# Four of twelve normalisation factors taken to all rows through memory instead of by PE's products and DVE's copy

## The reference

```python
def rms_norm(x, g, eps=EPS):
    xf = x.astype(jnp.float32)
    y = xf * lax.rsqrt(jnp.mean(xf * xf, axis=-1, keepdims=True) + eps)
    return (y * g.astype(jnp.float32)).astype(x.dtype)

def sq_relu_mlp(hn, w_up, w_down):
    return jnp.square(jax.nn.relu(hn @ w_up)) @ w_down
...
    ckv = hn @ w_dkv                                  # mla_shared_kv, hn = rms_norm(h, kv_in_norm_g)
    c, k_rope = ckv[..., :KV_LORA], ckv[..., KV_LORA:]
    kv = (rms_norm(c, kv_norm_g) @ w_ukv).reshape(B, S, MLA_HEADS, MLA_NOPE + MLA_V)
...
    cq = rms_norm(hn @ w_dq, q_norm_g)                # mla_attention
    q = (cq @ w_uq).reshape(B, S, H, MLA_NOPE + MLA_ROPE)
...
        h = h + sq_relu_mlp(rms_norm(h, mlp_norm_g[l]), w_up[l], w_down[l])
```

## Time and profile before

| | us |
|---|---|
| median of 3 runs | 1815.76 (1815.21 to 1815.92) |
| the profiled execution, its own time | 1815.61 |
| its span, first to last instruction | 1813.5 |
| PE busy | 1799.1 (99% of the span) |
| DVE busy | 879.6 (48%) |
| ACT busy | 623.7 (34%) |
| POOL busy | 536.9 (30%) |

### The profile page before, as it was taken

How to read it: one execution, slowest core, us unless ns; L and a number is a source line. 1 busy time by engine, 2 the same in 40 slices (tenths; PEclk the granted TensorE clock), 3 DMA queues, 4 the chain that set the end, 5 groups by cost and what they waited for, 6 DMA issues and landing times.

```text
span 1813.5 us, 21889 instructions
## 1 busy us (share of the span) xinstructions
PE 1799.1 (99%) x8494; PEld 1462.4 (81%) x8496; DVE 879.6 (48%) x1223; ACT 623.7 (34%) x916; POOL 536.9 (30%) x340
## 2 busy tenths in 40 slices
PE   9999999999999999999999999999999999999999
PEld 8877788888888887788888888877677888888877
DVE  6556563333334767553333334479655422333357
ACT  4344532222222345422222224334645332221244
POOL 1222254132325530153232225423222220210232
PEclk9999999999999999999999999999999999999999
DMA  5322222222322234325222322322122222232222
GB/s 211 108 84 78 75 93 93 93 93 93 104 97 100 79 108 131 111 93 128 93 93 94 114 93 89 115 81 70 55 92 97 93 93 93 93 116 86 100 95 92
DMA packets 37058, 177.70 MB, mean 98 GB/s; under 512 B 4569, under 2 KB 11513, under 8 KB 18041
## 3 DMA queue, kind: packets, MB, share of 16 engines
q1 hardware_dynamic: 35808, 175.06, 28.7%
q10 hardware_dynamic: 1176, 1.63, 0.7%
HBM read 161.99 MB, written 3.67 MB: 91 GB/s over the span
## 4 chain that ended last, share of the span: by engine, by line
PE 88%; DVE 8%; ACT 2%; issue 1%; POOL 1%; DMA 0%; SPq 0%; DVEq 0%; ACTq 0%; POOLq 0%
PE ps L564 23%; PE ps L565 22%; PE ps L566 22%; PE ps L619 3%; PE ps L618 3%; PE ps L596 3%; PE ps L830 1%; PE ps L792 1%; DVE wlo L1751 1%; PE ps L841 1%; DVE idx_score L2223 1%; DVE top L2221 1%; PE ps L638 1%; PE ps L1010 1%; PE ps L1020 1%
## 5 line engine op out<-in xcount | busy, mean ns | idle before, releaser
L1751 DVE TENSOR_TENSOR wlo<-raw,whi 128x2048 fp32r<-128x2048 f32 x133 | 325.8, 2449 | 301.6 <-ACT whi L1249 301.1
L564 PE MATMUL ps<-xb,whi 128*128 128x512 f32 (+1 forms) x996 | 388.4, 390 | 1.4 <-ACT probs L1553 0.8
L566 PE MATMUL ps<-xb,wlo 128*128 128x512 f32 (+1 forms) x996 | 386.1, 388 | 0.0
L565 PE MATMUL ps<-xb,whi 128*128 128x512 f32 (+1 forms) x996 | 386.1, 388 | 0.0
L1249 ACT ACTIVATE whi<-raw 128x2048 fp32r<-128x2048 f32 x143 | 273.0, 1909 | 324.6 <-PE ps L566 248.9
L564 PE MATMUL ps<-xa_hi,whi 128*128 128x512 f32 x788 | 308.5, 391 | 0.7 <-ACT probs L1318 0.7
L566 PE MATMUL ps<-xa_hi,wlo 128*128 128x512 f32 x788 | 306.8, 389 | 0.0
L565 PE MATMUL ps<-xa_lo,whi 128*128 128x512 f32 x788 | 306.7, 389 | 0.0
L564 PEld LDWEIGHTS ps<-xb,whi 128*128 128x128 f32 x996 | 187.1, 188 | 43.6 <-issue 5.0
L566 PEld LDWEIGHTS ps<-xb,wlo 128*128 128x128 f32 x996 | 187.0, 188 | 38.6
L565 PEld LDWEIGHTS ps<-xb,whi 128*128 128x128 f32 x996 | 187.1, 188 | 37.4
(11 more groups left out here) (332 smaller groups left out, 2428.3 us busy)
## 6 DMA issues: line engine op xcount, KB each, us to landing
raw<-wst SPq DMA_DIRECT2D x148, 1024.0 KB, 4.8
stage<-qk_raw SPq DMA_DIRECT2D x32, 128.0 KB, 2.3
mla_qn<-q_nope SPq DMA_DIRECT2D x8, 256.0 KB, 2.4
mla_v<-v_tok SPq DMA_DIRECT2D x8, 256.0 KB, 2.7
outT<-h SPq DMA_DIRECT2D x7, 256.0 KB, 2.0
h<-xT SPq DMA_DIRECT2D x3, 512.0 KB, 7.4
bias_scratch<-bias_rows ACTq DMA_DIRECT2D x1, 1536.0 KB
raw<-wst SPq DMA_DIRECT2D x4, 256.0 KB, 6.0
```

Of the source, the lines that this page charges most:

```text
L564: pe.matmul(out, lhs_hi, rhs_hi, start=first, stop=False)
L565: pe.matmul(out, lhs_hi, rhs_lo, start=False, stop=False)
L566: return pe.matmul(out, lhs_lo, rhs_hi, start=False, stop=last)
L1751: dve.tensor_tensor(wlo[slot][:, :], raw[slot][:, :], whi[slot][:, :].bitcast(F32), ALU.subtract).then_inc(wlo_done, 1)
```

## The change

For norms 1, 2, 4 and 5, `broadcast` is left out of PE's list and `take_rstd` out of DVE's. In their place ACT begins two transfers, with a wait ahead of each: `factor_away(n)` waits for `rstd_t` of norm n and writes its 128 x 4 numbers to 512 consecutive places of a row `factors` in memory; `factor_back(n)` waits until that has landed and reads the row back to all 128 rows of `rstd_f`. DVE's `factor_ready(n)` waits until this has landed. In `mlp` DVE's `mean_square` moves ahead of the `lo` of the third chunk. The other eight norms are as they were; their counts of `bc_done` and `rstd_f_done` are renumbered.

```diff
+BY_MEMORY = (1, 2, 4, 5)
+        factors = nc.dram_tensor("factors", (len(BY_MEMORY), S), F32, kind="Internal").ap()
...
@@ PE, mlp
                 def one_round(r, first):
                     for u in range(4):
-                        hook = None
-                        if first and u == 1:
-                            hook = lambda k: broadcast(norm) if k == 4 else None
-                        elif first and u == 2 and rows:
+                        if first and u == 2 and rows:
                             bias_by_distance()
...
@@ PE, dkv and ukv
             stat(2)
-            features((c + 1) % 2, c + 1, t + 2, xa_hi, xa_lo, hook=lambda k: broadcast(2) if k == 4 else None)
+            features((c + 1) % 2, c + 1, t + 2, xa_hi, xa_lo)
...
                     mm.then_inc(tile_done, 1)
-            broadcast(4)
...
@@ ACT
+            def factor_away(n):
+                act.wait_ge(rstd_t_done, n + 1)
+                act.dma_start(factors[BY_MEMORY.index(n), :].rearrange("(q p) -> p q", p=P), rstd_t[:, 4 * n:4 * n + 4],
+                              allow_slow_non_contiguous=True).then_inc(factor_out, 16)
+
+            def factor_back(n):
+                j = BY_MEMORY.index(n)
+                act.wait_ge(factor_out, 16 * (j + 1))
+                act.dma_start(rstd_f[:, :], factors[j:j + 1, :].to_broadcast([P, S])).then_inc(factor_in, 16)
...
@@ ACT, mlp
                         if first and u == 0:
                             hi(c + 2, 0, t + 2)
+                            factor_away(norm)
+                            factor_back(norm)
...
@@ ACT, dkv and ukv
             hi(c + 2, 0, t + 2)
+            factor_away(2)
+            factor_back(2)
...
             for q in range(QT):
+                if q == 1:
+                    factor_away(4)
+                elif q == 3:
+                    factor_back(4)
...
@@ DVE
+            def factor_ready(n):
+                dve.wait_ge(factor_in, 16 * (BY_MEMORY.index(n) + 1))
...
@@ DVE, mlp
                         if first and u == 0:
+                            mean_square(norm, D)
                             lo(c + 2, c % 2)
-                            mean_square(norm, D)
-                            take_rstd(norm)
+                            factor_ready(norm)
...
@@ DVE, dkv and ukv
             mean_square(2, D)
-            take_rstd(2)
+            factor_ready(2)
...
             lo(c + 2, c % 2)
-            take_rstd(4)
+            factor_ready(4)
```

More of the change, by code:

```diff
@@ L80 @@
 STATS = [n if n < 7 else n - 1 for n in range(N_NORMS)]
+BY_MEMORY = (1, 2, 4, 5)
+BY_PE = (0, 3, 6, 7, 8, 9, 10, 11)
+COPIED = (0, 3, 6, 7, 9, 11)
 QKV_STEPS = range(5, 12)
@@ L394, in build @@
         rows_stored = sem("rows_stored")
+        factor_out = sem("factor_out")
+        factor_in = sem("factor_in")
         nbias_full = sem("nbias_full")
@@ L715, in late_rstd, with linear @@
                     stat(norm)
-                elif k == (4 if norm == 0 else 6):
-                    if norm == 0:
-                        pe.wait_ge(const_loaded, 16 * len(consts))
+                elif k == 4:
+                    pe.wait_ge(const_loaded, 16 * len(consts))
                     broadcast(norm)
-            def linear(stage, pairs, xhi, xlo, fresh, norm=None, hook=None):
+            def linear(stage, pairs, xhi, xlo, fresh, hook=None):
                 c, t = C[stage], T[stage]
                 features(c % 2, c, t, xhi, xlo, fresh=fresh, hook=hook)
-                features((c + 1) % 2, c + 1, t + 2, xhi, xlo,
-                         hook=(lambda k: late_rstd(norm, k)) if norm is not None else None)
+                features((c + 1) % 2, c + 1, t + 2, xhi, xlo)
                 with pe.Fori(1, pairs) as i:
@@ L742, in one_round @@
                     for u in range(4):
-                        hook = None
-                        if first and u == 1:
-                            hook = lambda k: broadcast(norm) if k == 4 else None
-                        elif first and u == 2 and rows:
+                        if first and u == 2 and rows:
                             bias_by_distance()
-                        features((c + u) % 2, c + u + 8 * r, t + 2 * u, xhi, xlo, per=16, i=r, hook=hook,
+                        features((c + u) % 2, c + u + 8 * r, t + 2 * u, xhi, xlo, per=16, i=r,
                                  fresh=(xh_done, xl_done, x0) if first and u == 0 else None)
@@ L1070, in final_rstd @@
                 if k == 4:
-                    pe.wait_ge(rstd_f_done, 7)
+                    pe.wait_ge(rstd_f_done, COPIED.index(6) + 1)
                     broadcast(6)
@@ L1406, in residual, with mlp @@
                         x_hi(dst[:, 2 * u + a, :], h[:, 2 * u + a, :], gname(2 * u + a))
-            def mlp(stage, hhi, dst, gname, rows=False):
+            def mlp(stage, norm, hhi, dst, gname, rows=False):
                 c, t = C[stage], T[stage]
@@ L1443, in _ @@
             residual("wo_a", xa_hi, gains_of("mlp0"), ahead=True)
-            mlp("mlp0", xb_hi, xa_hi, gains_of("kv_in"))
+            mlp("mlp0", 1, xb_hi, xa_hi, gains_of("kv_in"))
             c, t = C["dkv"], T["dkv"]
@@ L1518, in _ @@
             residual("wo_b", xb_hi, gains_of("mlp1"))
-            mlp("mlp1", xa_hi, xb_hi, lambda k: g_x2[:, k:k + 1], rows=True)
+            mlp("mlp1", 5, xa_hi, xb_hi, lambda k: g_x2[:, k:k + 1], rows=True)
             c, t = C["w_in"], T["w_in"]
@@ L1677, in take_rstd @@
             def take_rstd(n):
-                act.wait_ge(bc_done, n + 1)
+                act.wait_ge(bc_done, BY_PE.index(n) + 1)
                 act.activation(rstd_f[:, :], BC[:, :], ACT.Copy).then_inc(rstd_f_done, 1)
@@ L1788, in take_rstd @@
             def take_rstd(n, dst=None):
-                dve.wait_ge(bc_done, n + 1)
+                dve.wait_ge(bc_done, BY_PE.index(n) + 1)
                 dve.tensor_copy((rstd_f if dst is None else dst)[:, :], BC[:, :]).then_inc(rstd_f_done, 1)
-                dve.wait_ge(rstd_f_done, n + 1)
+                dve.wait_ge(rstd_f_done, COPIED.index(n) + 1)
+            def factor_ready(n):
+                dve.wait_ge(factor_in, 16 * (BY_MEMORY.index(n) + 1))
             def tile_ready(t, per=0, i=0):
@@ L2413, in pair @@
                             lo_halves(c + 2, (1,))
-                            dve.wait_ge(rstd_f_done, 9)
+                            dve.wait_ge(rstd_f_done, COPIED.index(9) + 1)
                         tt = t + 2 * s
@@ L2463, in _ @@
             lo_halves(c + 2, (1,))
-            dve.wait_ge(rstd_f_done, 10)
+            dve.wait_ge(rstd_f_done, COPIED.index(11) + 1)
             for u in range(4):
```

## The result

| | us |
|---|---|
| before, median of 4 runs | 1815.49 (1814.56 to 1815.92) |
| after, median of 4 runs | 1846.17 (1845.53 to 1846.71) |
| ratio | 1.017 (95% interval 1.0152 to 1.0187) |
| profiled execution's span, before and after | 1813.5 and 1844.5 |

The change costs 30.7 us, 1.7%. The forecast was 1814.8, and the time is far outside its range: of the rivals only C, the slow store, points this way, and it stopped at 1828.9.

What follows compares the result with a forecast made beforehand. PE was taken to bound both MLPs, DVE the stage dkv and the end of ukv. -1.8 + 1.2 - 0.4 = -1.0 us on 1815.61 gave 1814.6, with the median 0.15 higher 1814.8 us; range 1812.0 to 1818.0.

Steps and rivals of the forecast that it cites:

- C: All four places: each 4-byte store piece costs what a 1536-byte piece of `bias_rows` does; +13.1 us, 1828.9; chance 0.11.
- the price of the store: Store of the factors: 1.7 us plus 0.05 us a piece, 32 pieces for each DMA engine, 3.3 us.
- the upper end of 9.1 us: Store of the factors: 1.7 us plus 32 pieces an engine at 0.23 us, the price from `bias_rows`.
- T: Where norms go through memory: time from ACT's first issue to DVE's release; 6.1 us, ends 4.1 and 11.9.
- first MLP: PE-bound first MLP: PE sheds one broadcast and the transfers stay covered; -0.90 us.
- dkv: DVE-bound stage dkv: DVE's first reading comes later and PE's saved 0.90 is lost; +1.2 us.
- end of ukv: DVE-bound end of ukv: tables done earlier, low part then starts when ACT's high part ends; -0.4 us.
- second MLP: PE-bound second MLP: PE sheds one broadcast and the transfers stay covered; -0.90 us.
- the way back: Read of the row to all 128 rows: 2.7 us with DMA engines free, possibly 4.8 beside a weight load.
- the cover: In the MLPs: longest T before PE waits for a bank; 8.8 us in the first, 9.7 in the second.
- the point at dkv: Stage dkv: the time the transfers may take for no change, separating gain from loss; 4.9 us.
- One bound: Stage dkv with short T: no better than about -1.1 us, as PE's own list allows 0.90 + 0.18.

Runs made afterwards that it cites:

- e1: Transfers alone, none of the reference's work: 512 neighbouring 4-byte pieces land in 8.1 us, 64 bytes apart in 2.6, 128 pieces of 16 bytes in 1.4.
- d_line: One store form run alone: 512 pieces of 4 bytes spaced 64 bytes apart in memory; 2.6 us.
- e3: Changed kernel with 26 useless PE products added ahead of the third chunk in each MLP; 1841.19 us, ratio 1.0139.
- e4: Changed kernel without its four factor stores and the wait for their landing, so the factors read back are wrong; 1811.38 us, ratio 0.9976.
- e7: Changed kernel with the store in 16-byte pieces, DVE reading the factor row at a 16-byte step, PE's sums untouched; 1817.98 us, ratio 1.0015.
- e8: Changed kernel with only norms 1 and 5 by memory, 16-byte store pieces and DVE's stepped reading; 1814.98 us, ratio 0.9995.
- e9: Transfers alone, none of the reference's work: 1 MB load beside each transfer; load 7.0 us beside the 4-byte store, 5.9 beside the 16-byte one.
- e2: Changed kernel with PE gathering every fourth token, so the store has 128 pieces of 16 bytes; 1815.95 us, ratio 1.0004.

## Why the prediction was wrong

**The step that failed** is the price of the store: "I take 0.05 us a piece, near the low end because a piece carries 4 bytes and not 1536", 3.3 us in all. Measured: 9.3 to 11.3 in the kernel. A price by the piece was the wrong form too. Bytes, pieces and engines were what I looked at, and by them 2 KB is nothing; but the cost lies in where in memory the pieces go (e1: 8.1 or 2.6 us for the same 512 pieces). No row of the kernel before could give that number, as no store there has neighbouring pieces of 4 bytes. With that, the upper end of 9.1 us was no bound, and the range, which left out even that end by giving C 0.11, was too narrow. The rule of the Trainium skill (DMA: Bandwidth & Descriptors, Rules for kernel authors) against a last dimension that isn't contiguous pointed the right way, and I gave it no weight of its own; but the rule doesn't tell the slow stores from the quick ones, as `d_line` breaks it too and lands in 2.6.

**The rest of the working, with the measured times put in:**

| place | forecast | its formula with the measured T | measured |
|---|---|---|---|
| first MLP | -0.9 | 15.4 - 8.8 - 0.9 = +5.7 | +7.6 |
| dkv | +1.2 | 14.3 - 4.9 = +9.4 | +11.2 |
| end of ukv | -0.4 | +5.0 | +4.7 |
| second MLP | -0.9 | 15.6 - 9.7 - 0.9 = +5.0 | +7.8 |
| sum | -1.0 | +25.1 | +31.3 |

At the end of ukv: the issue stands with the second take-out, and 9.28 + 5.68 us later the row is back, 15.0 after that take-out, where the tables before started 10.0 after it (657.72 and 667.73). Between dkv and this stretch 0.6 us come back.

**What the formula lacks** is the clock. PE's wait of 6.5 us is 5.7 of the first MLP's 7.6; the other 1.9 are the products after it at 1.2 GHz. In the second MLP it is 5.1 and 2.7. e3 shows it: with PE at work through the wait the clock stays, 1.8 us go in the first MLP, and in the second 1.7 net of a wait of its own. For dkv (9.4 of 11.2) the half clock stands in the windows from 636 to 645 too, but there it wasn't tested apart. At the end of ukv PE stood for 3.2 us before 696.2 and the clock read 0.57 from 696 to 700, with no loss beyond the formula's. A rival that has PE stand for several us must carry this; C didn't, and that is some 6 of the 17 us by which it fell short, the store and the way back being the rest.

**What was right.** An MLP gives 0.90 us if T is under the cover: 0.92, 0.93 and 0.92 in e4, e7 and e8. 4.9 us is the point at dkv: 9.4 us of shift at DVE's first `ckv` for a T of 14.3, to 0.1. DVE sets the pace there, so that a slower DVE reading (e7) costs what PE sheds. C's mechanism, PE waiting for a bank behind DVE behind the store, is what happened, and its tell, a wait of PE for `u_tmp` in the third chunk, is in the trace. One bound was too tight: for a short T I gave dkv at most 1.1 us, and e4 has 1.5.

**The way back** was put at 2.7 where the engines are free, and 4.8 beside a load. e1 has 3.0 and e9 5.9, both longer, and the changed kernel 3.2 to 5.7: small errors beside the store's.

**Is there a version that wins?** e4, whose T no real store can have (1.4 us for the quickest store, and the way back), is 0.24% faster than before. Of those that compute everything, e2, e7 and e8 land between 0.9995 and 1.0015. In each of them what PE sheds comes back elsewhere: in PE's own sums (e2), in DVE's readings (e7), in a late chunk (e8). I have found none that beats the kernel before by more than can be measured. Putting the order right on the way back, with the 16-byte store and a read from memory in steps, was not tried.

## What to carry to other kernels

Before a few numbers per row go to memory, see where they land: 512 pieces of 4 bytes, sixteen to each 64 bytes, cost 8 us and more, the same bytes as 16-byte pieces 1.4 (4.4 beside a load of 1 MB). Loads of another queue begun behind such a store hardly moved until it was nearly through. Where a forecast hangs on a transfer that the trace doesn't have, the honest range is set by how wrong its form can be, not by the nearest row; one run with the transfer alone would have shown 8 us in place of 3.3. And PE's two waits of about 6 us cost 1.9 and 2.7 us beyond their length, by the products that followed at half the clock.

## What the runs showed of the hardware that I had not expected

- A store of 512 neighbouring 4-byte pieces lands after some 8 us alone (once 9.3, in the kernel once 11.0) and up to 12.3 beside a load; 8 bytes apart 3.2, 64 bytes apart 2.6, 512 bytes apart 1.8; as 128 pieces of 16 bytes 1.4, or 4.4 beside a load of 1 MB. Where nothing runs beside it, the DMA engines record nothing in most of that time.
- A load of 1 MB begun 1.5 us behind such a store takes 12.5 to 12.8 us in place of 4.8. Begun 1.5 to 6.8 us behind, it lands 13.7 to 14.4 us after the store's start and 2.9 to 5.4 after its landing. Begun a hair ahead of the store, it takes 5.9 to 7.3.
- Beside the store of `bias_rows` (1.5 MB in pieces of 1536 bytes) a load of 1 MB takes 19.1 to 19.3 us, in the kernel before as in the others.
- Two kilobytes read to all 128 rows take 3.0 us alone and 5.9 beside a load of 1 MB.
- DVE with one 32-bit operand at a step of 16 bytes takes 1.07 us for 128 x 512 in place of 0.69 (e7); PE with weights at that step 1.80 us for its eight short products in place of 0.95 (e2).
